# Rounding and rest of every split weight chunk moved to GpSimd

## The reference

```
def swiglu(h, w1, w2):
    gate, up = jnp.split(h @ w1, 2, axis=-1)
    return (jax.nn.silu(gate) * up) @ w2

def modulate(h, shift, scale):
    return h * (1.0 + scale[:, None, :]) + shift[:, None, :]
```

## Time and profile before

| | us |
|---|---|
| median of 3 runs | 4071.24 |
| lowest, highest | 4070.95, 4079.08 |
| span of the profiled execution, first to last instruction | 4077.1 |

### The profile page before, as it was taken

The page is one execution under the profiler, slowest core; times in us unless marked ns, Lnnn a source line. Parts: engine busy times, 40 slices in busy tenths (PEclk is TensorE's granted clock), DMA queues, the critical chain, the costliest instruction groups (busy, mean ns, idle before and its releaser), DMA issues. The chain is left out here.

```text
span 4077.1 us, 35826 instructions
## 1 busy us (share of the span) xinstructions
PE 3536.0 (87%) x12594; PEld 2393.3 (59%) x12594; DVE 1910.2 (47%) x2585; ACT 1105.3 (27%) x1425; POOL 77.1 (2%) x148
## 2 busy tenths in 40 slices
PE   4997889999789998858999963999979679989987
PEld 1444468877458787523888521588847347558433
DVE  5756266536358824243664498366333433143001
ACT  1221243233432214211442101244242322132000
POOL 0000000000000000000000000000000000000000
PEclk9897999999899999868999986999989889999988
DMA  5331146522035532101333210233323112222111
GB/s 211 96 123 53 42 153 192 188 83 73 16 119 196 172 99 79 52 0 52 93 97 96 69 47 11 73 98 95 96 81 100 36 48 86 82 63 97 52 62 62
DMA packets 100408, 360.85 MB, mean 89 GB/s; under 512 B 11152, under 2 KB 11169, under 8 KB 100065
## 3 DMA queue, kind: packets, MB, share of 16 engines
q1 hardware_dynamic: 77936, 276.07, 21.1%
q0 software_dynamic: 20080, 75.27, 5.7%
q10 hardware_dynamic: 2304, 8.39, 0.5%
HBM read 357.59 MB, written 2.10 MB: 88 GB/s over the span
## 5 line engine op out<-in xcount | busy, mean ns | idle before, releaser
L1583 DVE TENSOR_TENSOR weight_lo<-weight_ring,weight_hi 128x1024 fp32r<-128x1024 f32 (+1 forms) x390 | 468.7, 1204 | 931.5 <-ACT weight_hi L1104 927.5
L1104 ACT ACTIVATE weight_hi<-weight_ring 128x1024 fp32r<-128x1024 f32 (+1 forms) x390 | 406.9, 1045 | 1266.0 <-PE proj_banks L683 926.3
L683 PE MATMUL proj_banks<-h_hi,weight_hi 128*128 128x512 f32 x1584 | 617.2, 390 | 9.6 <-DVE weight_lo L1583 9.6
L683 PE MATMUL proj_banks<-h_lo,weight_hi 128*128 128x512 f32 x1584 | 617.0, 389 | 0.0
L683 PE MATMUL proj_banks<-h_hi,weight_lo 128*128 128x512 f32 x1584 | 616.9, 389 | 0.0
L640 PE MATMUL proj_banks<-h_tiles,weight_ring 128*128 128x512 f32 x768 | 348.2, 616 | 62.1 <-DVE scratch L1591 38.3
L1617 DVE RECIPROCAL scratch<-scratch 128x512 f32<-128x512 f32 (+1 forms) x39 | 129.2, 3312 | 479.9 <-ACT scratch L1104 479.9
L683 PEld LDWEIGHTS proj_banks<-h_hi,weight_hi 128*128 128x128 f32 x1584 | 297.8, 188 | 73.5 <-issue 11.6
L683 PEld LDWEIGHTS proj_banks<-h_lo,weight_hi 128*128 128x128 f32 x1584 | 297.6, 188 | 61.9
L683 PEld LDWEIGHTS proj_banks<-h_hi,weight_lo 128*128 128x128 f32 x1584 | 297.8, 188 | 61.5
L640 PE MATMUL proj_banks<-scratch,weight_ring 128*128 128x512 f32 x640 | 294.9, 624 | 27.0 <-DMA weight_ring<-in_w_dnr 27.0
(11 more groups left out here) (256 smaller groups left out, 4277.8 us busy)
## 6 DMA issues: line engine op xcount, KB each, us to landing
weight_ring<-in_w_up SPq DMA_DIRECT2D x176, 512.0 KB, 3.6
ada_ring<-in_ada POOLq DMA_DIRECT2D x96, 512.0 KB, 3.8
weight_ring<-in_w_dn SPq DMA_DIRECT2D x64, 512.0 KB, 3.5
weight_ring<-in_w_br SPq DMA_DIRECT2D x32, 512.0 KB, 3.6
weight_ring<-in_w_upr SPq DMA_DIRECT2D x32, 512.0 KB, 3.5
weight_ring<-in_w_dnr SPq DMA_DIRECT2D x32, 512.0 KB, 4.4
scratch<-in_ada POOLq DMA_DIRECT2D x24, 512.0 KB, 4.6
weight_ring<-in_w_dn SPq DMA_DIRECT2D x32, 384.0 KB, 3.1
```

Source lines behind the costliest of these rows:

```text
L683: last = mm(proj.banks[:, u % RING, :], stationary(split0 + n)[:, w], moving(k), start=k + m == 0, stop=k == kt - 1 and m == 2)
L1104: return nc.scalar.activation(out, in_, func, **kw)
L1583: return v.tensor_tensor(out, a, b, op)
```

## The change

GpSimd now does both instructions for every one of the 390 chunks: `tensor_copy` from the slot to `weight_hi`, a wait on `w_rounded`, and `tensor_tensor` with subtract to `weight_lo`. It does them stage by stage in program order (`split_stage`, `split_up`). The rings, semaphores, sizes and waits for PE's use stay as they were. ACT and DVE lose these instructions. Their loops over `br` and `upr`, which had a last turn of their own, run all turns in one loop.

The modulation rows are written out in groups of four. Eight groups stand before the first split, one more at the wait on `gla_ready`. In the loops of `up0` and `up1` a group of four rows is issued after every fourth chunk. In `dn0`, after its fourth chunk, stand the loads of `pool_w` and of two condition vectors, and the group of rows for `up1`. The loads of `ctx`, `grid`, `dist`, `dft`, `sgu_w` and `sgu_b` keep their waits and stand between the stages' splits.

```diff
-    def modulation(first, count):
...
-        with pool.Fori(1, count // ADA_RING) as i:
-            for q in range(ADA_RING):
-                pool.wait_ge(s["ada_used"], i * ADA_RING + (first + q - ADA_RING + 1))
...
+    def modulation_rows(group):
+
+        for row in range(4 * group, 4 * group + 4):
+            if row >= ADA_RING:
+                pool.wait_ge(s["ada_used"], row - ADA_RING + 1)
+            pool.dma_start(c.ada_slot(row), d["ada"][len(FIRST_ROWS) + row]).then_inc(c.ada_landed[row % ADA_RING], 16)
+
+    def split_chunk(name, n):
+
+        split, chunk = c.first_split[name] + n, c.first_chunk[name] + (n if name != "br" else 4 * (n // 3) + n % 3)
+        w = chunk_floats(name, n)
+        if split >= SPLIT_RING:
+            pool.wait_ge(*split_use(c, split - SPLIT_RING))
+        pool.wait_ge(*c.chunk_landed(chunk))
+        nc.gpsimd.tensor_copy(c.hi(split)[:, 0:w], c.slot(chunk)[:, 0:w]).then_inc(s["w_rounded"], 1)
+        pool.wait_ge(s["w_rounded"], split + 1)
+        nc.gpsimd.tensor_tensor(c.lo(split)[:, 0:w], c.slot(chunk)[:, 0:w], c.hi(split)[:, 0:w].bitcast(F32), ALU.subtract) \
+            .then_inc(s["w_split"], 1)
...
+    def split_up(name, group):
+
+        for n in range(2 * FT):
+            split_chunk(name, n)
+            if n % 4 == 3:
+                modulation_rows(group + n // 4 + 1)
+
+    split_up("up0", 8)
+    for n in range(4):
+        split_chunk("dn0", n)
     pool.dma_start(c.pool_w, d["pool_w"]).then_inc(s["pool_loaded"], 16)
...
-    modulation(80, 48)
+    modulation_rows(20)
+    split_stage("dn0", 4)
+    for name in ("cu", "sq", "sk", "sv"):
+        split_stage(name)
+    split_up("up1", 20)
+    for name in ("dn1", "mqk", "mv", "mo", "up2", "dn2", "up3", "dn3"):
+        split_stage(name)
     pool.wait_ge(*c.proj.filled(("dn3", 7)))
...
+    split_stage("rk")
+    for name in ("rq", "rv", "fv", "ru", "rg"):
+        split_stage(name)
+    for n in range(SPLIT_RING):
+        split_chunk("br", n)
     pool.wait_ge(*c.mix.filled(("rs", 3, 5)))
...
+    split_stage("br", SPLIT_RING)
+    split_stage("upr")
...
             st.done(f(T(squares_at(r) + k), X(k), ACT.Square), s["sq_ready"])
-            if r in SPLIT_UP and k == KD - 2:
-
-                up = SPLIT_UP[r]
-                for n in range(SPLIT_RING):
-                    round_chunk(up, n)
...
                 act.wait_ge(proj.full_sem, i * 4 + u + 1)
-                round_ahead(up, i, j)
...
                 ada_in_loop(i, j, layer, ctx)
-                rest_ahead(up, i, j)
```

More of the change, by code:

```diff
@@ L1121, in round_h @@
         st.done(f(c.norm_hi(r, k), H(k), ACT.Copy), s["h_rounded"])
[L1123 to L1144, removed]
     def norm(r):
@@ L1494, in scalar_program, with gate_tiles @@
     u0 = proj.number[("br", 0)]
-    def gate_tiles(i, last=False):
+    def gate_tiles(i):
         for n in range(2):
@@ L1500, in gate_tiles @@
                 act.wait_ge(proj.full_sem, i * 12 + u + 1)
[L1501 to L1505, removed]
                 act.wait_ge(proj.empty_sem[(u + 3) % RING], i * 3 + ((u + 3) // RING - 2))
                 f(T(24 + 3 * n + g), proj.banks[:, u % RING, :], ACT.Sigmoid).then_inc(proj.empty_sem[u % RING], 1)
-    with act.Fori(0, 3) as i:
+    with act.Fori(0, 4) as i:
         gate_tiles(i)
-    gate_tiles(3, last=True)
     def post_norm(stage, r, y):
@@ L1524, in scalar_program, with relu_tiles @@
     u0 = proj.number[("upr", 0)]
-    def relu_tiles(i, last=False):
+    def relu_tiles(i):
         for j in range(4):
@@ L1529, in relu_tiles @@
             act.wait_ge(proj.full_sem, i * 4 + u + 1)
-            if not (last and j >= 2):
-                round_ahead("upr", i, j)
             act.wait_ge(s["mlp_mid"], i * 4 + j + 1)
             f(T(32 + j), proj.banks[:, u % RING, :], ACT.Relu).then_inc(proj.empty_sem[u % RING], 1)
-    with act.Fori(0, F3T // 4 - 1) as i:
+    with act.Fori(0, F3T // 4) as i:
         relu_tiles(i)
-    relu_tiles(F3T // 4 - 1, last=True)
     post_norm("dnr", 1, 32)
 SPLIT_UP = {1: "up0", 2: "cu", 3: "up1", 4: "mqk", 5: "up2", 7: "up3", 10: "upr"}
-R_CHUNKS = [(name, n) for name in ("rk", "rq", "rv", "fv", "ru", "rg") for n in range(splits_of(STAGE[name]))] + [("br", 0), ("br", 1)]
 def chunk_floats(name, n):
@@ L1953, in vector_program @@
     r4 = lambda i: T(i)[0:4, :]
-    for n in range(8 + SPLIT_RING, 24):
-        rest_m(n)
     st.link(v.memset(r4(27), 1.0))
@@ L2098, in vector_program @@
     st.done(v.tensor_reduce(small[:, 96:112], T(41, 2).rearrange("p (g c) -> p g c", c=64), AX.X, ALU.add), s["vs_var"])
-    for n in range(16 + SPLIT_RING, 22 + SPLIT_RING):
-        rest_r(n)
     dve.wait_ge(s["vs_std"], 1)
@@ L2142, in vector_program, with branch_tiles @@
     u0 = proj.number[("br", 0)]
-    def branch_tiles(i, last=False):
+    def branch_tiles(i):
         for n in range(2):
             out = c.pool[:, bass.ds(i * (2 * S) + (16 + n) * S, S)]
-            for g in range(3):
-                ahead = 3 * n + g + SPLIT_RING
-                if not (last and ahead >= 6):
-                    split, chunk = c.first_split["br"] + ahead, c.first_chunk["br"] + 4 * (ahead // 3) + ahead % 3
-                    dve.wait_ge(s["w_rounded"], i * 6 + (split + 1))
-                    tt(c.lo(split), c.slot(chunk), c.hi(split).bitcast(F32), ALU.subtract).then_inc(s["w_split"], 1)
             for g in range(3):
@@ L2163, in branch_tiles @@
                     dve.wait_ge(sem, i * 2 + (n + 1))
-    with dve.Fori(0, 3) as i:
+    with dve.Fori(0, 4) as i:
         branch_tiles(i)
-    branch_tiles(3, last=True)
     def post_norm(stage, r, y, gain, sem):
@@ L2179, in vector_program, with square_tiles @@
     u0 = proj.number[("upr", 0)]
-    def square_tiles(i, last=False):
+    def square_tiles(i):
         for j in range(4):
             u = u0 + j
-            if not (last and j >= 2):
-                rest_ahead("upr", i, j)
             dve.wait_ge(proj.empty_sem[u % RING], i + (u // RING + 1))
             tt(c.pool[:, bass.ds(i * (4 * S) + j * S, S)], T(32 + j), T(32 + j), ALU.mult).then_inc(s["mlp_mid"], 1)
-    with dve.Fori(0, F3T // 4 - 1) as i:
+    with dve.Fori(0, F3T // 4) as i:
         square_tiles(i)
-    square_tiles(F3T // 4 - 1, last=True)
     post_norm("dnr", 1, 32, 8, s["out_ready"])
```

77 lines of the change are left out of this document (8 added, 69 removed).

## The result

| | us |
|---|---|
| changed kernel, median of 4 runs | 4115.90 |
| lowest, highest | 4111.61, 4119.57 |
| kernel before, median of 4 runs | 4071.97 |
| ratio, 95% interval | 1.0101, 1.0087 to 1.0115 |
| profiled execution: span, its own time | 4112.9, 4114.67 |

The change costs 1.0%, 44 us. Predicted were 4125 us, and 4095 to 4165 us as the forecast's own range. So differences of a few us between stages, read from one profile of each kernel, are no firmer than that.

A forecast was written before the change was run, and what follows sets the result against it. PE, busy 87% of the span, was taken as the bound. Terms of -15.2 + 54 + 11 + 3.5 = +53 us gave 4130 us profiled, 4125 us predicted; own range 4095 to 4165 us, with both signs 4052 to 4225.

The forecast's parts named there:

- second sum: Whole kernel if DVE and GpSimd hinder one another on SBUF: +53 us, with 54 in up1 and 11 in up0.
- Full exclusion: Up0 and up1, both engines reading two SBUF operands: one waits until the other's instruction is over; 5.4 us a turn in up1.
- Rivals B and C: GpSimd's chunk slower, 5.0 us, giving 4190 us, chance 0.20; or faster, 2.5 us, giving 4046 us, chance 0.09.
- first sum: Whole kernel if DVE and GpSimd don't hinder one another: -9.2 us, including +6 us in up1 from the rows' order.
- first pairs: After first pairs of chunks, PE waits 1.9 us at seven places, 13.3 us against 11.3 before: +2.0 us.
- Dn1's wait of 6.75 us: At dn1, PE's wait behind DVE's eight modulation products goes, with the slow matmuls after it: -9.0 us.
- The banks' 8.1 us: Token or head stages, PE waiting for banks that ACT empties: roundings ahead of four copies go, -4.2 of 8.1 us.
- The last norm: At the last norm, two roundings of 2.01 us ahead of the last square leave the chain: -2.0 us.
- Sq and sk: In sq and sk, five PE waits where ACT and DVE were late in their own order go: -3.4 us.
- Up0: In up0 under full exclusion, GpSimd's chunk ends at 11.9 against 10.86 us, ten times: 11 us added.
- Rival A: Whole kernel, no hindrance between DVE and GpSimd: 4062 us, chance 0.18.
- Rival D: DVE's or ACT's waits move onto another semaphore; gains of dn1, banks and last norm fail to appear: 4077 us, chance 0.03.

The follow-up runs named there:

- e2: Changed kernel with the modulation rows in up0 and up1 spread, two behind a turn's fourth chunk and one behind each of the next two; 4109.6 us.
- e3: Changed kernel with up1's DVE products taking their second operand from PSUM instead of SBUF (other numbers multiplied); 4106.1 us.
- e1: Changed kernel with up1 and dn1's first two chunks rounded by ACT and subtracted by DVE again; 4063.2 us, 0.9975 of the kernel before.
- e5: Changed kernel with both rows spread in up0 and up1 and up1's products reading PSUM; 4063.4 us, 0.9973 of the kernel before.
- e6: Changed kernel with ACT rounding again in up1 and for dn1's first two chunks, GpSimd only subtracting there; 4090.8 us.

## Why the prediction was right

**The second sum's mechanism held, at a smaller size.** Up1 and dn1 were to cost 54 - 9 + 1.5 = 46.5 us; they cost 43.3. That the two agree so well is in part luck. At the last tile of up1 DVE's step is 46.6 us late against the norm before, not 54, and dn1 gives back 3.3 us, not 7.5: its first chunks make PE wait 2.38 and 0.58 us, where I had 1.5. A wait in each turn, lengthened products and lengthened GpSimd instructions were all there, and up2 and up3 kept their pace (-0.7 us from up2 to dn3). The working through one turn gave 5.4 us, 3.4 of waiting and 2.0 of slow matmuls; measured are 4.2. PE's waits between 1250 and 1400 us are 17.8 us, 3.1 a turn of 26 (each 2.4 to 4.0 us, where I had named 3 us or more), which leaves 1.1 for slow matmuls and what a listed wait leaves out, at a granted clock of 0.95. The term for the slow matmuls was the one mis-sized. And I had let only chunk 4 be late. There is no such single place: e2 moved chunk 4 forward and the turn stayed at 25.8 us. The limit is the sum over the turn, which I did not form; it needs only counts and the durations with GpSimd's pair.

**Full exclusion, not half.** I took the dearer end for want of a row. It was right for the products, CAST, `mid_lo` and COPY of up1, also for those I had not counted: the COPY of four columns was 1417 ns in the mean. It is not right for all that reads and writes SBUF. At the norms in sq and sk six RECIPROCALs run beside GpSimd for 2.2 to 3.0 us each and all list their 3.35 us of before, for instance (DVE, then GpSimd, in the kernel after):

```profile
961.53 3.35 DVE L1579 RECIPROCAL scratch<-scratch 128x512 f32<-128x512 f32 x1 [2.00 <-ACT scratch L1139]
```

```profile
961.82 1.04 POOL L572 CAST weight_hi<-weight_ring 128x1024 fp32r<-128x1024 f32 x1 [2.84 <-PE proj_banks L738]
962.94 2.39 POOL L574 TENSOR_TENSOR weight_lo<-weight_ring,weight_hi 128x1024 fp32r<-128x1024 f32 x1
```

The Trainium skill, "SBUF — State Buffer", section "Who interferes with whom", by whose rule the second sum was the one to hold, agrees with these rows in its two-input case: the second product of a row, with both operands in SBUF, lists 1590 ns, and e3's, with one operand in PSUM, 1221 ns beside GpSimd's work.

**A chunk on GpSimd: 3.7 us predicted, 3.38 and steps measured**, with CAST 1.04 and subtraction 2.34 us undisturbed, 3.44 in the mean of up2. The subtraction is 1.91 times DVE's 1.226. The Trainium skill, "GPSIMD Engine Reference", section "Elementwise — side-by-side cycle accounting", gives 1.96 for an add of 2048 fp32 columns; the trace agrees within 3%. Rivals B and C fell with this: it is under 4.07 us and over 3.1.

**Terms of the first sum.** The first pairs' seven waits are 2.3, 2.2, 2.7, 1.9, 1.9, 1.9 and 2.2 us, 15.0 against 11.3: +3.7 instead of +2.0. Where they are above 1.9, a DVE instruction stands beside the pair and GpSimd's subtraction or CAST is longer, as 3.20 us ahead of up1 (the 2.7). Dn1's wait of 6.75 us is gone, with 3.0 us of new waits in its place; e1, whose up1 is as before, shows -7.4 us with a wait of 1.3 us left, against -9.0. The banks' 8.1 us went whole, not by half. mqk to mo gave 5.0 us and rk to rg 4.6, with rk's wait at 5.6 us instead of 4.5 (+1.1; predicted +1.4). The last norm gave 1.0 us at its RECIPROCAL, of 2.0. Sq and sk: the shift at their RECIPROCALs is -5.0 us, but most of it is lost again before the norm of up1, where the stage sum of cu to norm is +2.1. It was largely off the critical path.

**Up0: 11 us predicted, 4.0 measured.** Four of the eleven were there, by the order of the rows (e2), and the spread rows took all of them. My walk had DVE's instructions in up0 wait in full behind each GpSimd one; with 5.0 instead of 10.1 us of products a turn they found room. The walk also has a slip: 14.2 less two products of 1.26 is 11.7, not 11.9, which makes 8 to 9 us of the 11.

**How near the sum came.** For the profiled execution it said 4130 us; that took 4112.9, 17 us less. The median missed by 9 us only, largely because the 5.9 us that I took off for the profiled execution before does not apply to the one after. That part of the agreement is luck.

**Cu: a stage that I had at about 2 us.** Its shift is +3.8 us at the first RECIPROCAL behind it (948 us before), 1.4 of it in the first pair. For the rest I see DVE's convolution, whose tiny instructions wait for GpSimd's to end; that it is all of the rest is not shown. DVE, then GpSimd, in cu after; 16 columns take 2.01 us, to 926.89, where GpSimd's subtraction ends at 926.87:

```profile
924.88 2.01 DVE L1545 TENSOR_TENSOR scratch<-scratch,others 128x16 f32<-128x16 f32 x1
...
932.80 0.17 DVE L1545 TENSOR_TENSOR scratch<-scratch,others 128x16 f32<-128x16 f32 x1
```

```profile
924.20 2.67 POOL L574 TENSOR_TENSOR weight_lo<-weight_ring,weight_hi 128x1024 fp32r<-128x1024 f32 x1
```

**Rival A** (4062) is what e5 is: with the coupling and the order gone, 4063 us. **Rival D** is refuted by e1, where the gains outside up1 all appear.

## What to carry to other kernels

Where DVE and GpSimd both work from SBUF, add up over one turn of a loop what each has of instructions that exclude one another, as if it were one engine, and compare the sum with the bounding engine's turn; idle time of either engine is no room. Which they are has to be read from a trace: here those with two operands in SBUF, CAST and COPY, and not RECIPROCAL. Where the sum is well below and no order of waits ties the engines (e3 shows that one can), moving work to GpSimd was free (up2, up3); where it was well above, all of it was paid (25.9 worked out, 25.8 and 26.0 measured), and at 21.8 against 21.76 the pace was unstable. And when an edit that should free a loop gives little, try it together with the edit for the next limit before dropping either: here 6 and 10 us apart were 52 together.

## What the runs showed of the hardware

- DVE's instructions of a few columns can wait as long as large ones: COPY of 128x4 lists 1417 ns in the mean of up1, a TENSOR_TENSOR of 16 columns 2.01 us in place of 0.17.
- Some one-input DVE instructions from SBUF to SBUF are hindered like the two-input ones (CAST of 128x512, 1051 ns in the mean for 0.43), and some are not (RECIPROCAL of 128x512, 3.35 us beside GpSimd and alone). Two-input ones with one operand in PSUM are not (688 ns and 1221 ns, as before).
- GpSimd's one-input CAST, 1.04 us for 1024 columns, is as fast as ACT's rounding (1.06), and counts in the sum: e6, without it, has turns of 23.8 us for 26.0.
- One program showed two stable paces, 21.76 and 23.7 us a turn, at a sum of 21.8 against PE's 21.76.
